# Hybrid encoder block: row norms from the transposed input, matmuls on made-up data at the start, a finer cut end, and the scan's products in three fp32r passes

## The reference

```
h    = rms_norm(x, g_mix);  proj = h @ w_in      # z | xBC | dt_f, dt_b | q | k | v | gate_a | gate_b
y_ssm  = SSD scan of silu(conv5(xBC)), forward and backward, 8 groups of 4 heads of 64,
         state 128, chunks of 128;  + d_skip * x,  * silu(z),  grouped rms_norm
y_attn = softmax attention, 16 query heads and 4 key heads of 128, rms-normed q and k, rotary
x    = x + (sigmoid(gate_a) * (y_ssm @ w_ssm_up) + sigmoid(gate_b) * (y_attn @ w_attn_up)) @ w_out
x    = x + square(relu(rms_norm(x, g_mlp) @ w_mlp_in)) @ w_mlp_out
out  = rms_norm(x, g_final)
```

## Time and profile before

| | us |
|---|---|
| median of 3 runs | 1664.09 (1662.59 to 1665.1) |
| the profiled execution | 1664.59 |
| its span, first to last instruction | 1663.0 |
| PE busy | 1639.3 |
| DVE busy | 1037.2 |
| ACT busy | 841.2 |
| POOL busy | 62.9 |

### The profile page before, as it was taken

How to read it: one execution, slowest core, us unless ns; L and a number is a source line. 1 busy time by engine, 2 the same in 40 slices (tenths; PEclk the granted TensorE clock), 3 DMA queues, 4 the chain that set the end, 5 groups by cost and what they waited for, 6 DMA issues and landing times.

```text
span 1663.0 us, 20066 instructions
## 1 busy us (share of the span) xinstructions
PE 1639.3 (99%) x8022; PEld 1381.4 (83%) x8022; DVE 1037.2 (62%) x1256; ACT 841.2 (51%) x1158; POOL 62.9 (4%) x59
## 2 busy tenths in 40 slices
PE   6999999999999999999999999999999999999998
PEld 5888888888888888888888888888888888888886
DVE  4777677777666677776565555545655556455554
ACT  5566566656565445454444544444543445335543
POOL 0000000000000134000000000000000000000000
PEclk9999999999999999999999999999999999999999
DMA  8566656666556664445575656666566566665563
GB/s 300 170 195 193 191 187 200 198 199 186 183 183 185 191 187 153 141 148 177 185 235 178 215 177 201 191 192 189 184 195 193 175 202 191 195 192 185 182 203 131
DMA packets 135565, 314.26 MB, mean 189 GB/s; under 512 B 10480, under 2 KB 11056, under 8 KB 135344
## 3 DMA queue, kind: packets, MB, share of 16 engines
q1 hardware_dynamic: 130608, 304.04, 58.2%
q10 hardware_dynamic: 4864, 8.94, 2.1%
HBM read 310.78 MB, written 2.16 MB: 188 GB/s over the span
## 4 chain that ended last, share of the span: by engine, by line
PE 94%; DVE 2%; DMA 1%; issue 1%; ACT 1%; SPq 0%; POOL 0%; POOLq 0%; ACTq 0%; DVEq 0%
PE G L1250 19%; PE G L1252 19%; PE G L1251 19%; PE S L1258 7%; PE G L1258 7%; PE S L1251 4%; PE S L1250 4%; PE S L1252 4%; PE S L1260 4%; PE G L1260 4%; PE S L1268 1%; DMA raw<-in_w_in 1%; PE S L1352 1%; DVE wlo L727 1%; PE S L1357 0%
## 5 line engine op out<-in xcount | busy, mean ns | idle before, releaser
L425 ACT ACTIVATE whi<-raw 128x1024 fp32r<-128x1024 f32 x556 | 589.5, 1060 | 730.5 <-PE G L1252 428.2
L727 DVE TENSOR_TENSOR wlo<-raw,whi 128x1024 fp32r<-128x1024 f32 x556 | 673.8, 1225 | 377.4 <-ACT whi L425 377.0
L1250 PE MATMUL G<-whi,a_both 128*128 128x512 f32 x960 | 381.8, 398 | 9.9 <-DVE a_both L760 9.2
L1252 PE MATMUL G<-whi,a_both 128*128 128x512 f32 x960 | 375.5, 391 | 0.0
L1251 PE MATMUL G<-wlo,a_both 128*128 128x512 f32 x960 | 375.2, 391 | 0.0
L1250 PEld LDWEIGHTS G<-whi,a_both 128*128 128x128 f32 x960 | 181.4, 189 | 47.4 <-DVE a_both L760 9.2
L1252 PEld LDWEIGHTS G<-whi,a_both 128*128 128x128 f32 x960 | 181.2, 189 | 38.4
L1251 PEld LDWEIGHTS G<-wlo,a_both 128*128 128x128 f32 x960 | 181.5, 189 | 36.9
L1250 PE MATMUL G<-whi,b_hi 128*128 128x512 f32 x480 | 187.5, 391 | 0.0
L1251 PE MATMUL G<-wlo,b_hi 128*128 128x512 f32 x480 | 187.2, 390 | 0.0
L1252 PE MATMUL G<-whi,b_lo 128*128 128x512 f32 x480 | 187.0, 390 | 0.0
(11 more groups left out here) (193 smaller groups left out, 1422.1 us busy)
## 6 DMA issues: line engine op xcount, KB each, us to landing
raw<-in_w_in SPq DMA_DIRECT2D x208, 512.0 KB, 4.2
raw<-in_w_mlp_in SPq DMA_DIRECT2D x128, 512.0 KB, 3.7
raw<-in_w_mlp_out SPq DMA_DIRECT2D x128, 512.0 KB, 4.6
raw<-in_w_ssm_up SPq DMA_DIRECT2D x32, 512.0 KB, 3.7
raw<-in_w_attn_up SPq DMA_DIRECT2D x32, 512.0 KB, 4.4
raw<-in_w_out SPq DMA_DIRECT2D x32, 512.0 KB, 4.2
segs<-cum_rows ACTq DMA_DIRECT2D x16, 512.0 KB, 9.3
gates<-in_x SPq DMA_DIRECT2D x8, 512.0 KB, 8.2
```

Of the source, the lines that this page charges most:

```text
L425: act.activation((whi_end if end else whi)[:, slot, 0:width], raw[:, slot, 0:width], ACT.Copy).then_inc(hi_made, 1)
L727: dve.tensor_tensor((wlo_end if end else wlo)[:, slot, 0:width], raw[:, slot, 0:width], (whi_end if end else whi)[:, slot, 0:width].bitcas ...
L1250: pe.matmul(out_ap, hi[:, k, cols], w_hi, start=start, stop=False)
L1252: return pe.matmul(out_ap, lo[:, k, cols], w_hi, start=False, stop=stop)
```

## The change

The norm of x no longer reads x. ACT squares `xt_raw`, the turned copy that is there already, in four instructions of 1024 columns (two in piece 3, two in piece 4 of window 0, behind the splits of these pieces). POOL adds the 16 blocks of squares in a chain of eight additions, seven of 512 columns and one of 256, each waiting for the one before. PE, after piece 7, waits for the last of them and sums over the partitions with two small plain fp32 matmuls against a column of -0.5. DVE reads that from PSUM. The four `load_x` DMAs at the start are gone (the loads of x ahead of `out` stay).

DVE fills a tile with two values at the start, and PE multiplies it with itself `WARM` = 6 times (plain fp32, 512 columns) ahead of its first real matmul.

In the scan, ACT makes a rounded high part and DVE a low part of each operand of the three products (`tm`, `xd`, the decays `mw`, the state `st`, and C as `ct`), and each product becomes three fp32r passes. The state product moves from after piece 3 to after piece 4, the product with the other chunk's state from after piece 6 to after piece 7, and the two halves of the decays move from pieces 2/3 and 4/5 to 1/3 and 2/4 on ACT (2 and 4 to 2 and 3 on DVE). ACT's first step of `zgate` now waits for the last scan product.

At the end, the last add, its squares and the closing multiplications are cut in two, the fixed part of the row sum is formed earlier, and the stores of a block are cut finer (`FIN_CUTS`).

```diff
+WARM = 6
+FIN_CUTS = (0, 640, FIN, 1664)
...
             for p in range(PIECES):
...
-                if (r, par) == (0, 0) and p >= 5:
-                    load_x(p - 5)
-                if (r, par, p) == (0, 1, 0):
-                    load_x(3)
...
@@ ScalarE, rates @@
-            if p == 5:
-                for c in range(4):
-                    act.wait_ge(s_x[c], 16)
-                for tb in range(TB):
-                    act.activation(squares[:, tb, :].rearrange("p (c n) -> p c n", c=4), x_sb[:, :, tb, :],
-                                   ACT.Square, accum_out=x_ss[:, tb:tb + 1]).then_inc(sq_x, 1)
+            if p in (3, 4):
+                for j in range(2 * p - 6, 2 * p - 4):
+                    act.activation(squares[:, 4 * j:4 * j + 4, :], xt_raw[:, 4 * j:4 * j + 4, :], ACT.Square
+                                   ).then_inc(xt_sq, 1)
@@ ScalarE, scan @@
                 for tb in range(TB):
                     act.activation(tm[:, tb, :], S[:, tb, 0:3 * P], ACT.Copy).then_inc(tm_made, 1)
-            if p in (2, 4):
-                half = p // 2 - 1
+                for tb in range(TB):
+                    act.activation(tm_hi[:, tb, :], S[:, tb, 0:3 * P], ACT.Copy).then_inc(tm_hi_made, 1)
+            if p == 1:
+                if not first(g):
+                    act.wait_ge(off_mm, g)
+                act.activation(ct_hi[:, :], cs[:, 3, :], ACT.Copy).then_inc(ct_hi_made, 1)
+            if p == 2:
+                act.wait_ge(scan_v, g * SCAN_V + 3)
+                act.activation(xd_hi[:, :, :], xd[:, :, :, :].rearrange("p c h d -> p c (h d)"), ACT.Copy
+                               ).then_inc(xd_hi_made, 1)
+            if p in (1, 2):
+                half = p - 1
                 act.wait_ge(s_segs[half], 16 * (g + 1))
...
-            if p in (3, 5):
-                half = p // 2 - 1
+            if p in (3, 4):
+                half = p - 3
...
-            if p == 4:
+            if p == 5:
                 act.wait_ge(st_mm, g + 1)
...
-                act.activation(st[:, :, :].rearrange("p a b -> p (a b)"), S[:, 3, :], ACT.Copy
+                act.activation(st_hi[:, :, :].rearrange("p a b -> p (a b)"), S[:, 3, :], ACT.Copy
                                ).then_inc(st_made, 1)
+                act.wait_ge(scan_v, g * SCAN_V + 4)
+                act.activation(mw_hi[:, :, :, :], mw[:, 0, :, :, :], ACT.Copy).then_inc(mw_hi_made, 1)
@@ ScalarE, end @@
         for tb in range(TB):
-            act.wait_ge(fin_v, FIN_V + 3 * tb + 1)
-            final_squares(3, tb)
+            for h in range(2):
+                act.wait_ge(fin_v, FIN_V + 5 * tb + 1 + h)
+                final_squares(3, tb, slice(h * T, (h + 1) * T), 3 + h)
...
+            for c in range(2):
+                cols = slice(FIN_CUTS[2 + c], (FIN_CUTS + (D,))[3 + c])
+                part = fin[:, tb, cols]
+                act.activation(part, part, ACT.Copy, scale=rstd_out[:, tb:tb + 1]).then_inc(fin_a, 1)
+                if tb == 1:
+                    act.wait_ge(fin_a, 3 + c)
+                    act.dma_start(o_k[:, tb, cols], part).then_inc(s_store, 16)
@@ VectorE @@
+        for e, value in enumerate((0.7853981, -1.6180339)):
+            dve.memset(tmp_a[:, 0, e:N:2], value).then_inc(set_warm, 1)
...
             if p == 7:
-                dve.wait_ge(sq_x, TB)
-                dve.tensor_scalar(x_var[:, :], x_ss[:, :], 1.0 / D, EPS, ALU.mult, ALU.add).then_inc(var_x, 1)
+                dve.wait_ge(xt_mm, 1)
+                dve.tensor_scalar(x_var[:, :], S[:, 3, 0:8 * TB:8], -2.0 / D, EPS, ALU.mult, ALU.add).then_inc(var_x, 1)
@@ VectorE, scan @@
+                dve.wait_ge(tm_hi_made, 2 * g + 2)
+                dve.tensor_tensor(tm_lo[:, :, :], tm[:, :, :], tm_hi[:, :, :].bitcast(F32), ALU.subtract
+                                  ).then_inc(tm_lo_made, 1)
...
+            if p == 3:
+                dve.wait_ge(xd_hi_made, g + 1)
+                dve.tensor_tensor(xd_lo[:, :, :], xd[:, :, :, :].rearrange("p c h d -> p c (h d)"),
+                                  xd_hi[:, :, :].bitcast(F32), ALU.subtract).then_inc(xd_lo_made, 1)
...
+            if p == 4:
+                dve.wait_ge(ct_hi_made, g + 1)
+                dve.tensor_tensor(ct_lo[:, :], cs[:, 3, :], ct_hi[:, :].bitcast(F32), ALU.subtract
+                                  ).then_inc(ct_lo_made, 1)
...
+            if p == 5:
+                dve.wait_ge(mw_hi_made, g + 1)
+                dve.wait_ge(scan_v, step(4))
+                dve.tensor_tensor(mw_lo[:, :, :, :], mw[:, 0, :, :, :], mw_hi[:, :, :, :].bitcast(F32), ALU.subtract
+                                  ).then_inc(mw_lo_made, 1)
+            if p == 6:
+                dve.wait_ge(st_made, g + 1)
+                dve.tensor_tensor(st_lo[:, :, :].rearrange("p a b -> p (a b)"), S[:, 3, :],
+                                  st_hi[:, :, :].rearrange("p a b -> p (a b)").bitcast(F32), ALU.subtract
+                                  ).then_inc(st_lo_made, 1)
@@ GpSimd, rates @@
+                def add(out_ap, first_ap, second_ap, n):
+                    pool.tensor_tensor(out_ap, first_ap, second_ap, ALU.add).then_inc(xt_sum, 1)
+                    pool.wait_ge(xt_sum, n)
+
+                total = tmp_b[:, :, 0:T]
+                pool.wait_ge(xt_sq, 1)
+                add(total, squares[:, 0:2, :], squares[:, 2:4, :], 1)
+                for j in range(1, 4):
+                    own = squares[:, 4 * j:4 * j + 2, :]
+                    pool.wait_ge(xt_sq, j + 1)
+                    add(own, own, squares[:, 4 * j + 2:4 * j + 4, :], 2 * j)
+                    add(total, total, own, 2 * j + 1)
+                add(tmp_b[:, 0, 0:T], tmp_b[:, 0, 0:T], tmp_b[:, 1, 0:T], 8)
                 pool.wait_ge(var_x, 1)
@@ TensorE @@
+        pe.wait_ge(set_warm, 2)
+        for _ in range(WARM):
+            pe.matmul(S[:, 0, :], tmp_a[:, 0, 0:P], tmp_a[:, 0, :], start=True, stop=True)
...
+            if p == 7:
+
+                pe.wait_ge(xt_sum, 8)
+                for tb in range(TB):
+                    last = pe.matmul(S[:, 3, 8 * tb:8 * tb + 8], tmp_b[:, 0, tb * P:(tb + 1) * P],
+                                     minus_half[:, :], start=True, stop=True)
+                last.then_inc(xt_mm, 1)
@@ TensorE, scan @@
-            if p == 3:
-                pe.wait_ge(scan_v, g * SCAN_V + 3)
+            if p == 4:
+                pe.wait_ge(tm_lo_made, g + 1)
+                pe.wait_ge(xd_lo_made, g + 1)
                 for c in range(TB):
-                    last = pe.matmul(S[:, 3, c * 4 * HD:(c + 1) * 4 * HD], tm[:, c, 2 * P:3 * P],
-                                     xd[:, c, :, :].rearrange("p h d -> p (h d)"), start=True, stop=True)
+                    last = three_passes(S[:, 3, c * 4 * HD:(c + 1) * 4 * HD], c, 2, tm_hi, tm_lo,
+                                        xd_hi[:, c, :], xd_lo[:, c, :], True, True)
                 last.then_inc(st_mm, 1)
             if p == 6:
-                pe.wait_ge(scan_v, g * SCAN_V + 4)
+                pe.wait_ge(mw_lo_made, g + 1)
                 for c in range(TB):
                     for h in range(4):
-                        last = pe.matmul(S[:, 2, (4 * c + h) * HD:(4 * c + h + 1) * HD],
-                                         mw[:, 0, h, c, :], tm[:, c, h * HD:(h + 1) * HD], start=True, stop=True)
+                        heads = slice(h * HD, (h + 1) * HD)
+                        last = three_passes(S[:, 2, (4 * c + h) * HD:(4 * c + h + 1) * HD], h, c, mw_hi_flat, mw_lo_flat,
+                                            tm_hi[:, c, heads], tm_lo[:, c, heads], True, True)
                 last.then_inc(y_mm, 1)
-                pe.wait_ge(st_made, g + 1)
+            if p == 7:
+                pe.wait_ge(ct_lo_made, g + 1)
+                pe.wait_ge(st_lo_made, g + 1)
                 for c in range(TB):
-                    last = pe.matmul(S[:, 3, c * 4 * HD:(c + 1) * 4 * HD], cs[:, 3, c * P:(c + 1) * P],
-                                     st[:, 1 - c, :], start=True, stop=True)
+                    last = three_passes(S[:, 3, c * 4 * HD:(c + 1) * 4 * HD], 0, c, ct_hi_row, ct_lo_row,
+                                        st_hi[:, 1 - c, :], st_lo[:, 1 - c, :], True, True)
                 last.then_inc(off_mm, 1)
```

105 lines of the change are left out of this document (67 added, 38 removed).

## The result

The changed kernel takes 1666.55 us (median of 20 runs, 1665.43 to 1668.1), the kernel before, run beside it, 1664.47 (20 runs, 1662.59 to 1665.62). The ratio is 1.0015 with a 95% interval of 1.0009 to 1.0021: slower by about 2.1 us (0.13%), less than the 0.2% that I had set as the bound of "no change", but 4.5 us above the forecast and above the range (1665.5). The profiled execution has a span of 1665.2 us, 2.2 above before's 1663.0.

The account below looks back on a forecast made before the run. PE bounds the kernel, busy 1639.3 of 1663.0 us. Start -6.95, scans +5.3 and end -0.3 make -1.95 against the profiled 1664.59: 1662.6, or 1662.1 for the median; range 1658.5 to 1665.5.

Parts of the forecast that it names:

- The mechanism of the made-up products: Start: six made-up products lift PE's clock near 5.9 us and end near 9; piece 0 takes 2.72 instead of 5.04 us.
- the wait at piece 3: Start: PE, now faster, would wait 1.0 us at piece 3 for low part 3, made at 18.40 us.
- both bounds: Start, landing of piece 6, forecast 24.2 us: 26.75 (nothing gained) or 22.5 (other x loads no longer compete).
- The stall at the turn: Window 0: PE's 5.5 us wait at the turn of the dt products, and the clock's fall after it, would disappear.
- The gain of the start: Piece 8 starts 8.0 us earlier; DVE's chain behind POOL's sum takes back 1.05 at low part 11; 6.95 us gained.
- the price of POOL's additions: Start: additions of 512 columns cost 1.31 us each, so the sum comes at 36.7 and PE idles 0.7 us.
- the second term: Scans: added work on DVE and ACT costs nothing; low parts 10 to 12 are done 1.1 us before DVE's first tap.
- the scan: Eight scans: short passes 0.115 us each (0.108 to 0.118), +0.66 us a group, +5.3 in all (3.9 to 5.8).
- Rival (e): Scans: fast fp32r weight loads make the inner product's 24 passes take 1.3 us; 13.6 us faster, 1650.5; chance 0.04.
- The end: After the last matmul: finer closing multiplications and stores gain 0.3 us, between 0 and 0.6.
- (c): Start: POOL's additions cost 2.74 instead of 1.31 us, the chain ends at 46.7; +10.2 us, 1674; chance 0.04.
- (d): Scans: DVE's cover fails, PE waits about 1 us in each of eight windows; +6 us, 1668; chance 0.06.

Follow-up runs that it names:

- low_short: Changed kernel with DVE's low parts of pieces 7, 8 and 9 made on 8 of 1024 columns only, the rest stale: 1664.93 us, before 1664.14.
- fill_gap: Changed kernel with ten plain fp32 products of 128 columns ahead of PE's wait for the sum: 1666.99 us, 1.0019 of before.
- three_pass: Changed kernel with POOL's eight additions on DVE and the scan's last product back behind the inner one: 1661.72 us, ratio to before 0.9988.

## Where the prediction was right and where it failed

**Right.** The mechanism of the made-up products and their end ("near 9 us"; 8.5), full speed for piece 0, the wait at piece 3 (0.90 against 1.0). Their matmuls are at full distance (0.43 for 512 columns in fp32) from 4.94 us on, 3.5 us after the first and not 4.6; as the real operands came at 9.3, nothing hung on it. Piece 6's split at 24.12, forecast 24.2, which excludes both bounds. The stall at the turn and its fall of the clock are gone.

**Right, and first seen in the experiments.** The gain of the start, -8.0 + 1.05 = -6.95: with the sum in time the first turn comes at 64.97, which is -7.16. `low_short` has piece 8 8.36 us earlier than before (36.81), and PE waits 1.47 us instead of before's 0.38 for low part 11: the 1.05 of DVE behind it measured 1.09.

**Failed, the term that carried the miss:** the price of POOL's additions in "7 x 1.31 + 0.75 + 8 handovers of 0.08 = 10.5, so the sum is there at 36.7". Three of the seven had to wait for a low part that DVE had begun before them, and their rows took 2.16: 4 x 1.29 + 3 x 2.16 + 0.72, with seven handovers of 0.08, make 12.9 us, from 26.28 to 39.18. I had asked how long an addition takes and not what it must wait for. The earlier trace rows held the answer. I had written that POOL "would run beside a busy DVE", and yet gave the 2.74 a chance of 4 in 100, as a slow price for all additions. In the trace of before, POOL's product at 172.61 ends 0.90 us after the DVE low part that was running when it began (171.80, 1.22 us), and so do the one of 1.57 us at 320.01 (0.89) and the one of 2.74 at 123.48 (0.90 after the low part of 124.11, 1.21 us; another DVE operation of 1.21 us ran ahead of that). So even the 1.31 held a wait of 0.4 us, and the 2.74 was the same operation behind two of DVE's. Why two of DVE's went ahead of POOL there, and one at a time here, no run shows.

Between the changed kernel and `low_short`, whose sum is in time, lie 3.53 us at the first turn: 0.82 for the clock (`fill_gap`), the other 2.7 for the late sum, through which DVE's whole chain is late.

The Trainium skill, GPSIMD Engine Reference, section 3.1, has 4497 ns for 2048 columns; the estimate of 1.12 us from it, a quarter, fits neither the 1.29 of an addition alone nor the 2.16. The measurements decide.

**Failed, the second term:** "They are done some 1.1 us before DVE's first tap can start ... So I cost both engines at nothing." The walk followed DVE to its own next consumer (and there it held: the first tap still had 1.55 us of idling in front of it) but not to the queue that its low parts release. I had asked of DVE's steps who waits for them on PE and ACT; SP waits for them too, and what changed was the order of two loads on two queues. It cost 1.36 us in the early groups of this execution (0.2 to 2.7 in the other kernels with this order) and 0.04 us in every group.

**Right, the scan.** Passes of 256 columns 0.118, the state product:

```profile
183.89 0.28 PE L1332 MATMUL S<-xd_hi,tm_hi 128*128 128x256 f32 x1
184.01 0.28 PE L1333 MATMUL S<-xd_lo,tm_hi 128*128 128x256 f32 x1
...
190.10 0.28 PE L1333 MATMUL S<-tm_lo,mw_hi 128*128 128x64 f32 x1
...
192.55 0.28 PE L1334 MATMUL S<-tm_hi,mw_lo 128*128 128x64 f32 x1
```

At 64 columns a pass takes (192.55 - 190.10) / 22 = 0.111 us, between my bounds of 0.108 and 0.118 and nearer to the lower one than the 0.115 that I took. 24 x 0.111 = 2.67, 0.94 more than the 1.73 of before; less 0.37 that makes 0.57 a group, and 0.60 was measured where 0.66 was forecast. Rival (e), cheap passes through faster loads of weights, did not happen: a pass costs what an fp32 record costs. The Trainium skill's section on Fast Weight Load (TensorE: Matmul & The Clock Gate) has faster loads where the type is not fp32; no such gain shows for fp32r here, where a load of 128 columns is recorded with 0.19 us in either type.

**The end:** -0.3, as forecast. In sum, with the two failed terms repaired, `three_pass` is 3.1 us under before in the spans and 2.1 in the medians, against the forecast -1.95; by the spans the scans were 0.8 us cheaper than forecast (8 x 0.56 instead of 5.3), so the match of the medians is in part luck. The change as made adds 3.5 us of missed gain, 1.4 us of early stalls and 0.04 us a group.

One slip in the chances: those of (c) and (d) add up to 0.10 and those of a faster kernel to 0.30, not to 0.09 and 0.29. Nothing else hangs on it.

## What to carry to other kernels

A product with few columns is paid by its matmuls, not by its columns: three passes instead of two fp32 records cost 0.90 us a group at 64 columns, while at 256 columns the same passes save 0.19 us a product. Take the duration of a moved operation from rows where the same neighbours work beside it, above all on POOL and DVE, and compare the ends of the rows of both engines: a row can hold a wait that the list of waits doesn't show. And follow a moved step through every queue that it releases, up to the DMA's order of issue: here a product put 3 us later on PE changed which of two loads went first.
